# Expert 0's tokens by an indirect gather instead of by products with a permutation, in a two-layer decoder trunk on one core

## The reference

```python
def moe_swiglu(h, w_router, w_gate, w_up, w_down):
    logits = (h @ w_router).astype(jnp.float32)
    top_v, top_i = lax.top_k(logits, TOP_K)
    top_w = jax.nn.softmax(top_v, axis=-1)
    gates = jnp.sum(jax.nn.one_hot(top_i, N_EXPERTS, dtype=jnp.float32) * top_w[..., None], axis=-2)
    ...
    for e in range(N_EXPERTS):
        y = y + gates[..., e:e + 1] * swiglu(h, w_gate[e], w_up[e], w_down[e])
    return y
```

## Time and profile before

| | |
|---|---|
| time, median of 3 runs | 1446.66 us (1445.18 to 1448.37) |
| the profiled execution's own time | 1444.75 us |
| its span in the trace | 1442.8 us |
| PE busy | 1412.0 us, 98% |
| DVE busy | 1110.6 us, 77% |
| ACT busy | 932.8 us, 65% |
| POOL busy | 43.3 us, 3% |
| moved from and to memory | 440.19 MB, 305 GB/s on the mean |

### The profile page before, as it was taken

How to read it: one execution, slowest core, us unless ns; L and a number is a source line. 1 busy time by engine, 2 the same in 40 slices (tenths; PEclk the granted TensorE clock), 3 DMA queues, 4 the chain that set the end, 5 groups by cost and what they waited for, 6 DMA issues and landing times.

```text
span 1442.8 us, 16731 instructions
## 1 busy us (share of the span) xinstructions
PE 1412.0 (98%) x6925; PEld 1184.6 (82%) x6925; DVE 1110.6 (77%) x839; ACT 932.8 (65%) x721; POOL 43.3 (3%) x48
## 2 busy tenths in 40 slices
PE   9999999999989999999999999999999999999997
PEld 7886788887978888888888888888888888888885
DVE  4785654546454888898988888888888898988896
ACT  3664534344353777777777777777777777777774
POOL 0000000000010000000000000000000000001000
PEclk9999999999999999999999999999999999999999
DMA  9743465554541899999999999999999999999992
GB/s 312 212 167 117 161 204 182 198 175 158 179 166 51 312 382 381 373 373 388 353 402 384 358 394 380 377 375 377 389 361 395 382 351 406 382 372 382 413 368 109
DMA packets 136849, 440.19 MB, mean 305 GB/s; under 512 B 11472, under 2 KB 28864, under 8 KB 121024
## 3 DMA queue, kind: packets, MB, share of 16 engines
q1 hardware_dynamic: 130688, 424.24, 79.4%
q0 software_dynamic: 3600, 13.12, 2.4%
q10 hardware_dynamic: 2480, 1.69, 0.4%
HBM read 433.25 MB, written 5.78 MB: 304 GB/s over the span
## 4 chain that ended last, share of the span: by engine, by line
PE 89%; DVE 6%; ACT 2%; DMA 1%; issue 1%; SPq 0%; POOL 0%; ACTq 0%; POOLq 0%; DVEq 0%
PE ps L1725 28%; PE ps L1727 28%; PE ps L1726 28%; PE ps L2245 2%; DVE lo L1103 2%; DMA wr<-in_od_w_router_dram 1%; ACT hi L710 0%; DVE work L1129 0%; DMA raw<-in_ev_w_in_dram 0%; PE ps L2165 0%; PE ps L2022 0%; PE ps L1785 0%; PE ps L1914 0%; DVE work L1293 0%; DVE negmax L1281 0%
## 5 line engine op out<-in xcount | busy, mean ns | idle before, releaser
L1103 DVE TENSOR_TENSOR lo<-raw,hi 128x2048 fp32r<-128x2048 f32 (+1 forms) x403 | 904.3, 2284 | 108.8 <-ACT hi L710 106.9
L710 ACT ACTIVATE hi<-raw 128x2048 fp32r<-128x2048 f32 (+1 forms) x403 | 770.5, 1916 | 260.0 <-PE ps L1727 248.7
L1725 PE MATMUL ps<-hi,xT_hi 128*128 128x512 f32 (+1 forms) x1200 | 470.9, 392 | 3.5 <-DVE xT_lo L1298 2.0
L1727 PE MATMUL ps<-hi,xT_lo 128*128 128x512 f32 (+1 forms) x1200 | 464.8, 387 | 0.0
L1726 PE MATMUL ps<-lo,xT_hi 128*128 128x512 f32 (+1 forms) x1200 | 464.2, 387 | 0.0
L1725 PEld LDWEIGHTS ps<-hi,xT_hi 128*128 128x128 f32 x1200 | 226.2, 189 | 51.5 <-DVE xT_lo L1298 3.5
L1727 PEld LDWEIGHTS ps<-hi,xT_lo 128*128 128x128 f32 x1200 | 225.6, 188 | 46.8
L1726 PEld LDWEIGHTS ps<-lo,xT_hi 128*128 128x128 f32 x1200 | 226.1, 188 | 43.7
L1725 PE MATMUL ps<-hi,hT_hi 128*128 128x512 f32 x536 | 210.2, 392 | 0.9 <-DVE hT_lo L1394 0.9
L1727 PE MATMUL ps<-hi,hT_lo 128*128 128x512 f32 x536 | 208.8, 390 | 0.0
L1726 PE MATMUL ps<-lo,hT_hi 128*128 128x512 f32 x536 | 208.6, 389 | 0.0
(11 more groups left out here) (270 smaller groups left out, 706.7 us busy)
## 6 DMA issues: line engine op xcount, KB each, us to landing
raw<-in_od_w_gate_dram SPq DMA_DIRECT2D x112, 1024.0 KB, 7.8
raw<-in_od_w_up_dram SPq DMA_DIRECT2D x112, 1024.0 KB, 8.4
raw<-in_od_w_down_dram SPq DMA_DIRECT2D x112, 1024.0 KB, 7.7
raw<-in_od_w_qkv_dram SPq DMA_DIRECT2D x12, 1024.0 KB, 5.2
raw<-in_ev_w_gate_dram SPq DMA_DIRECT2D x11, 1024.0 KB, 5.1
raw<-in_ev_w_up_dram SPq DMA_DIRECT2D x11, 1024.0 KB, 5.1
raw<-in_ev_w_down_dram SPq DMA_DIRECT2D x11, 1024.0 KB, 5.2
raw<-in_ev_w_in_dram SPq DMA_DIRECT2D x4, 1024.0 KB, 9.5
```

The source lines that it names most:

```text
L710: act.activation(unit(hi, n), unit(raw, n), ACT.Copy).then_inc(hi_ready, 1)
L1103: dve.tensor_tensor(unit(lo, n), unit(raw, n), unit(hi, n).bitcast(F32), ALU.subtract)\
L1725: pe.matmul(out, s_hi, m_hi, start=start, stop=False, skip_group_check=True)
L1727: return pe.matmul(out, s_lo, m_hi, start=False, stop=stop, skip_group_check=True)
```

## The change

Expert 0 gets its tokens as the other experts do. `pick_rows(0)` follows the placement products on TensorE, DVE casts the list (`copy_picked(0)`, between `make_place(0)` and the count), POOL's loop starts at expert 0, and `gather(0)` waits for the rows and turns them. TensorE branches first and then does 14 keepers, the eight transposes and four keepers, where it did the products, eight keepers and the branch. `copy_picked` is the code that stood in the loop; for the other experts it says the same as before.

```diff
             fits = few(pool)
             with pool.If(fits):
-                for e in range(1, NE):
-                    pool.wait_ge(picked_ready, e)
-                    if e > 1:
+                for e in range(NE):
+                    pool.wait_ge(picked_ready, e + 1)
+                    if e:
                         pool.wait_ge(gathered, 2 * e)
                     pool.indirect_dma_start(rows, None, normed_d, bass.IndirectOffsetOnAxis(ap=picked[:], axis=0))\
                         .then_inc(rows_landed, 16)
+                    if not e:
+                        continue
                     pool.wait_ge(y_copied, e)
...
+            def copy_picked(e):
+
+                dve.wait_ge(picked_done, e + 1)
+                if e:
+                    dve.wait_ge(rows_landed, 16 * e)
+                dve.tensor_copy(picked[:], ps[:, 6, SEQ:SEQ + 1]).then_inc(picked_ready, 1)
+
             dve.wait_ge(iota_ready, 4)
             make_place(0)
+            copy_picked(0)
             link(dve.tensor_copy(rcount[:], ps[:, 6, 32:40]))
...
                     if e + 1 < NE:
-                        dve.wait_ge(picked_done, e + 1)
-                        if e:
-                            dve.wait_ge(rows_landed, 16 * e)
-                        dve.tensor_copy(picked[:], ps[:, 6, SEQ:SEQ + 1]).then_inc(picked_ready, 1)
+                        copy_picked(e + 1)
...
             def gather(e):
 
+                pe.wait_ge(rows_landed, 16 * (e + 1))
                 if e:
-                    pe.wait_ge(rows_landed, 16 * e)
                     pe.wait_ge(g_silu_done, NCH * e)
-                    for k in range(KD):
-                        ins = pe.transpose(ps[:, 4 + k // 4, P * (k % 4):P * (k % 4) + P], rows[:, P * k:P * k + P], ident[:])
-                        if k % 4 == 3:
-                            ins.then_inc(gathered, 1)
-                    return
-                pe.wait_ge(place_ready, 1)
-                pe.wait_ge(xs_ready, 2 * 3 + T)
                 for k in range(KD):
-                    out = ps[:, 4 + k // 4, P * (k % 4):P * (k % 4) + P]
-                    for t in range(T):
-                        ins = pe.matmul(out, work[:, t, P * k:P * k + P], place[:, t, :], start=(t == 0), stop=(t == T - 1))
+                    ins = pe.transpose(ps[:, 4 + k // 4, P * (k % 4):P * (k % 4) + P], rows[:, P * k:P * k + P], ident[:])
                     if k % 4 == 3:
                         ins.then_inc(gathered, 1)
...
                 pe.wait_ge(place_ready, e + 1)
-                if e > 1:
-                    pe.wait_ge(picked_ready, e - 1)
+                if e:
+                    pe.wait_ge(picked_ready, e)
...
-            gather(0)
-            keep_busy(8, 7)
+            pick_rows(0)
             fits = few(pe)
             with pe.If(fits):
+                keep_busy(14, 7)
+                gather(0)
+                keep_busy(4, 7)
                 for e in range(NE):
```

## The result

The kernel after takes 1454.0 us (median of 5 runs, 1453.36 to 1455.8), the kernel before 1446.45 us beside it (5 runs, 1445.18 to 1448.37). The ratio is 1.0046, 95% interval 1.0032 to 1.0059: slower by 0.46%, or 7.55 us between the medians. The profiled execution took 1453.52 us, its span 1452.1.

The account below looks back on a forecast made before the run. TensorE's pace was taken to bound the kernel, the expert part having no slack. Path +6.9 and clock +2.0 gave +8.9 us, moving the 1446.66 us median to 1455.6, forecast as 1455.5 (+0.6%); 8 in 10 range 1451.0 to 1459.5.

Parts of the forecast that it names:

- The expert part has no slack: Behind 476 us: runs at TensorE's pace, so each microsecond expert 0's first gate product starts later lengthens the whole.
- The path, +6.9: From the router's result to expert 0's first gate product: it moves from 475.73 to 482.6 us, +6.9 us.
- list ready: Two small products on TensorE, 0.50 us, then DVE's cast of 0.15 us, ending at 471.05 us.
- count ready: On DVE, the count queues behind the list's cast and ends at 471.6 us, 1.1 us later than before.
- POOL's reading and branch: On POOL, between count and gather issue: 1.5 us, bounds 0.3 and 2.8, so issue at 473.1 us.
- issue to landing: Expert 0's 512 KB gather: 3.8 us calm transfer plus 2.8 for being a gather, 6.6 us; bounds 3.2 and 10.8.
- turns to gate: After the landing, turning and splitting the rows takes 2.8 us, 2.9 with the handover to TensorE.
- gate, behind `place`: Expert 0's first gate product, end of the new path, expected at 482.6 us where it was 475.73.
- The clock, +2.0: Around 480 to 486 us: granted clock falls to 0.5 to 0.6, costing 1.8 us plus 0.2 for turns.
- The clock holds: Rival, during the wait for the gather: keepers may suffice, so +6.9 us or less, 1453.6 us; chance 0.25.
- The landing is early: Rival, at the gather: rows land 475.1 to 475.7 us, gate +2.3 to +2.9, about 1449.3 us; chance 0.06.
- The landing is late: Rival, at the gather: full branch time and collision with weight loads, landing 484.0, +13.2 with clock, 1459.9 us; chance 0.11.

Follow-up runs that it names:

- loads_wait: The changed kernel, but SP holds back the first weight load the expert part frees until expert 0's rows have landed; ratio 1.0034, 1452.85 us.
- gather_first: The changed kernel, but POOL issues expert 0's gather once the list is there, ahead of reading the count and its branch; ratio 1.0056, 1455.67 us.
- after_again: The changed kernel, unchanged, run for a second profile; 1455.95 us.
- products_branch: The kernel before, but TensorE reads the count and branches ahead of expert 0's products, which are kept, keepers following inside the branch; ratio 1.0015.
- first_and_wait: The changed kernel with POOL's gather issued ahead of its branch and SP's next weight load held until the rows land; ratio 1.0055, 1454.84 us.

## Why the prediction was right, and where it was not

**The expert part has no slack: right.** From the first gate product to the output store it takes 961.54 and 961.55 us. The delay was passed on whole, in the changed kernel and in the variants; what two of them add is one more wait for weights in the last expert (0.5 and 0.7 us).

**The path, +6.9: right, 6.88 measured,** step by step:

| step | predicted | changed kernel's profile |
|---|---|---|
| list ready, behind `place`'s start | 1.6 | 1.55 |
| count ready | 2.15 | 1.98 |
| POOL's reading and branch | 1.5 (0.3 to 2.8) | 1.74 |
| issue to landing | 6.6 (3.2 to 10.8) | 6.7 |
| turns to gate | 2.9 | 2.67 |
| gate, behind `place` | 13.15 | 13.16 |

Two of these are right as sums and wrong as stories. I built the 6.6 us as 3.8 for the transfer in the calm and 2.8 for POOL's instruction, and set the weight load beside it at nothing. The instruction took 1.37 us and the load cost 2.2 (loads_wait). And I charged the branch as if taking it off would give it back; taking it off gave nothing (gather_first), since the instruction grows by nearly as much. List to landing is the firm quantity: 8.9 to 9.1 us with the weight load beside it, 6.3 to 6.8 without. That the single terms met the measured ones within 0.3 us, from ranges of 0.3 to 2.8 and 3.2 to 10.8, is in part luck.

**The clock, +2.0: the term that was mis-sized.** The clock did fall, but earlier than I said. I had it at 0.5 to 0.6 around 480 to 486 us, in the turns and the gate products; it was at 0.50 from 473.5 to 480.4 us, and at 1.00 when the turns and the gate began. What ran while it was low were keepers, and 14 of them at 0.43 us ended at 480.5, 1.0 us ahead of the rows. The price at the gate was nothing. The row I took it from the earlier trace rows had weight products in that place, here there were none. And even there the kernel had not lost the 1.8 us that I read. In the kernel before, the product at 139.27 us starts as soon as the low part of its weights is there. In after_again the clock did not fall at 136 us, and TensorE waited 1.34 us for the same low part. From the first dense product (134.91 in the earlier trace rows, 135.48 here) to this one it is 4.36 us in both; the fall cost the kernel 0.2 us behind it. Before, then after_again:

```profile
139.27 0.69 PE L1725 MATMUL ps<-hi,xT_hi 128*128 128x512 f32 x1
```

```profile
135.48 0.50 PE L1732 MATMUL ps<-hi,xT_hi 128*128 128x512 f32 x1 [0.55 <-DVE xT_lo L1300]
...
139.84 0.47 PE L1732 MATMUL ps<-hi,xT_hi 128*128 128x512 f32 x1 [1.34 <-DVE lo L1105]
```

"The clock holds", my first rival, gave +6.9 and 1453.6 us, and is nearer to the measured 1454.0 than my 1455.5, although the clock did not hold. Its reason was half right: the keepers pay, and without them the change costs 3.6 us more by the times, 2.8 of clock by the profiles.

**What I did not see:** that the clock falls ahead of `place` in many executions of either kernel. It moved `place` from 469.45 to 470.50 in the second profile of before; in the first of after, at 471.12, it is 0.96 of the 1.67 us. The 8.77 us between the two profiled executions (1444.75 and 1453.52) are 0.71 us that were there before 145 us already, 0.96 of clock ahead of `place`, 6.88 of path, 0.01 behind the gate, and 0.2 at the end. That I had 1453.65 for this execution is luck: 2.0 us of clock that cost nothing stood for 1.9 us of other things. A second such place lies at 338 us. There the clock fell in seven of the twelve profiles (after_again and every variant but gather_first and products_branch), and in these it did not fall at 136 us. It is not hidden behind a wait there: TensorE's work in after_again is 0.35 us later than in before at 335 us and 1.53 at 348, so it costs 1.2 us. None of the three profiles of kernels that keep the products has it, seven of the nine that gather do, and of the two profiles of the changed kernel one. Whether the edit makes this fall more frequent so few profiles can't tell.

The medians differ by 7.55, since runs of both kernels have such falls. Of the 7.55 some 6.9 are shown to be the path. The other 0.7 are within what the interval (1.0032 to 1.0059, 4.6 to 8.5 us) leaves open; the end of the program, the fall at 338 us and chance are candidates, and none of them is shown.

**The rivals.** "The landing is early" fell at 6.7 us of landing. Its page of the Trainium skill (DMA: Bandwidth & Descriptors, Anatomy of one DMA — SWDGE (gpsimd) path) has a formula by which 512 KB take an estimated 3.2 us; the best that a gather of this size did here was 4.5, with the engines free. So it does not hold for this gather, and the measurement decides. "The landing is late" needed a collision as with full engines; there was one, but with a single load, and it cost 2.2 us.

**The other side.** No variant of this design came near the kernel before. In the best the gate comes 10.99 us behind `place` (first_and_wait), against 6.28 for products that need no DMA.

## What to carry to other kernels

Here a gather through memory could not replace a few microseconds of products, at a place where TensorE had nothing else to do: from `place` to the gate it was 11 us even with free engines, and 6.3 with products. Ask first what else can run during the round trip. Keepers paid in this wait, but count them at the low clock too, since 14 that take 3.4 us took 6 there and became what was waited for in one profile. And before charging a fall of the clock with a price, ask what runs in it and what it waits for: it cost nothing over keepers, 0.2 us where a wait for weights hid it, and 2.8 us where it reached into the turns and the gate products. Last, break the difference of two profiles down by place before you explain it: two profiles of the same kernel differed by 2.6 us.

## What the runs showed of the hardware

- POOL's indirect gather of 128 rows of 4 KB takes 1.37 us as an instruction behind the count's reading and branch, and 2.70 to 2.81 us straight from a wait for the list. The landing behind the issue moves by as much: 4.5 or 5.9 to 6.0 us with free engines.
- Reading a number and branching, behind its release: 1.07 to 1.17 us on TensorE (after, products_branch), 1.74 on POOL (after, after_again, loads_wait).
- A 1 MB load issued 0.5 us behind the gather delays the landing by 2.2 us (6.7 and 4.5), and so does one issued 1.8 us behind it (8.1 in gather_first, 5.9 in first_and_wait). That is a little less than its own time at the 420 GB/s moved then, 2.5 us.
- TensorE's clock falls from 1.00 to 0.50 (2.4 to 1.2 GHz) in the router part in some executions and not in others, at instructions that are the same. In the kernel before that made 2.6 us between two profiles. A fall at 338 us, in seven of the twelve profiles, costs 1.2 us; one at 136 us costs 0.2, since a wait hides it.
- The program's end, from the output store's issue to the end of the span, takes 5.5 us in the three profiles in which expert 0 uses products and 6.3 to 6.6 in the nine that gather its rows, while the time outside the span falls from 1.95 to 1.42 us (first profiles). The net is 0.2 us. Nothing in the profile tells why.
